# Convolution sums of a two-layer block: 20 of 31 taps added by accumulating DMAs, ten as multiply-adds on VectorE

## What is computed

```python
h = rms_norm(x, g_pre_mix) * (1 + sc1) + sh1       # sc1, sh1: from c @ w_ada + b_ada
proj = h @ w_in                                    # u_glu, q, k, v, index q and k, gates
a, gt = split(u_glu); u = a * sigmoid(gt)          # 256 x 1024
u = conv(u, w_dw, width 31, causal, one filter per channel) + b_dw
y_conv = silu(layer_norm(u, g_ln, b_ln)) @ w_conv_out
y_attn = top-k sparse attention, 16 heads of 64, @ w_attn_out
x = x + gt1 * rms_norm((g_conv * y_conv + g_attn * y_attn) @ w_o)
```

## Time and profile before

| | |
|---|---|
| Time of the runs | 2699.56 us median of 3 (2699.01 to 2699.8) |
| The profiled execution: its own time | 2699.8 us |
| Its span, first to last instruction | 2698.0 us |
| Mean granted TensorE clock | 0.988 of 2.4 GHz |
| TensorE matmuls busy | 2584.3 us, 96% |
| VectorE busy | 1684.5 us, 62% |
| ScalarE busy | 1286.2 us, 48% |
| GpSimd busy | 3.4 us |
| DMA | 579.29 MB, of them 564.82 MB on the queue of the loads |

### The profile page before, as it was taken

The page is one execution under the profiler, slowest core; times in us unless marked ns, Lnnn a source line. Parts: engine busy times, 40 slices in busy tenths (PEclk is TensorE's granted clock), DMA queues, the critical chain, the costliest instruction groups (busy, mean ns, idle before and its releaser), DMA issues.

```text
span 2698.0 us, 28994 instructions
## 1 busy us (share of the span) xinstructions
PE 2584.3 (96%) x11660; PEld 2111.5 (78%) x11660; DVE 1684.5 (62%) x1914; ACT 1286.2 (48%) x1797; POOL 3.4 (0%) x10
## 2 busy tenths in 40 slices
PE   4999989999989999999999899999999999999998
PEld 3777767877868888888888787778788888888886
DVE  6899788988875555555555544666554454445455
ACT  4535666755454444444444454544454444444443
POOL 0000000000000000000000000000000000000000
PEclk9999999999989999999999999999999999999999
DMA  9888445777855556665554554345455555555553
GB/s 352 326 332 324 157 156 197 270 281 278 342 222 203 218 204 234 241 242 212 209 205 176 180 186 158 141 156 187 172 177 195 187 195 197 188 194 194 188 187 125
DMA packets 80566, 579.29 MB, mean 215 GB/s; under 512 B 8964, under 2 KB 8964, under 8 KB 10544
## 3 DMA queue, kind: packets, MB, share of 16 engines
q1 hardware_dynamic: 78480, 564.82, 57.8%
q10 hardware_dynamic: 1440, 9.81, 0.9%
q0 software_dynamic: 512, 2.81, 0.3%
HBM read 573.73 MB, written 3.67 MB: 214 GB/s over the span
## 4 chain that ended last, share of the span: by engine, by line
PE 76%; DVE 7%; ACT 3%; issue 1%; DMA 0%; ACTq 0%; DVEq 0%; SPq 0%
PE bank L640 72%; DVE wlo L1459 2%; PE bank L604 1%; ACT whi L965 1%; DVE raw L1469 1%; DVE X L1454 1%; DVE cv L1664 1%; ACT PR L965 0%; DVE SS L1454 0%; DVE cv L1454 0%; PE bank L752 0%; PE bank L800 0%; ACT SS L1335 0%; DMA raw<-in_w_in 0%; PE bank L885 0%
## 5 line engine op out<-in xcount | busy, mean ns | idle before, releaser
L1459 DVE TENSOR_TENSOR wlo<-raw,whi 128x1024 fp32r<-128x1024 f32 x882 | 1077.3, 1224 | 957.1 <-ACT whi L965 953.4
L965 ACT ACTIVATE whi<-raw 128x1024 fp32r<-128x1024 f32 x882 | 932.3, 1059 | 1289.2 <-PE bank L640 1169.2
L640 PE MATMUL bank<-whi,HTh 128*128 128x512 f32 x2560 | 706.2, 398 | 8.8 <-ACT HTh L965 5.8
L640 PE MATMUL bank<-wlo,HTh 128*128 128x512 f32 x2560 | 687.6, 391 | 3.5 <-DVE wlo L1459 3.5
L640 PE MATMUL bank<-whi,HTl 128*128 128x512 f32 x2560 | 689.2, 391 | 0.5 <-DVE HTl L1775 0.5
L640 PEld LDWEIGHTS bank<-wlo,HTh 128*128 128x128 f32 x2560 | 481.6, 188 | 106.4 <-DVE wlo L1459 4.8
L640 PEld LDWEIGHTS bank<-whi,HTl 128*128 128x128 f32 x2560 | 483.5, 189 | 103.7 <-DVE HTl L1775 1.0
L640 PEld LDWEIGHTS bank<-whi,HTh 128*128 128x128 f32 x2560 | 472.5, 189 | 113.9 <-issue 15.6
L1469 DVE CUSTOM_DVE_ANT_0 raw<-raw,GT,VECS 128x2048 f32<-128x2048 f32 x96 | 225.0, 2347 | 0.2 <-DMA raw<-in_w_ada 0.2
L640 PE MATMUL bank<-whi,ACTh 128*128 128x512 f32 x704 | 191.6, 394 | 0.0
L640 PE MATMUL bank<-wlo,ACTh 128*128 128x512 f32 x704 | 190.0, 392 | 0.0
(11 more groups left out here) (217 smaller groups left out, 1235.5 us busy)
## 6 DMA issues: line engine op xcount, KB each, us to landing
raw<-in_w_in SPq DMA_DIRECT2D x128, 1024.0 KB, 4.9
raw<-in_w_ada SPq DMA_DIRECT2D x96, 1024.0 KB, 6.5
raw<-in_w_gate SPq DMA_DIRECT2D x88, 1024.0 KB, 4.8
raw<-in_w_up SPq DMA_DIRECT2D x88, 1024.0 KB, 4.8
raw<-in_w_down SPq DMA_DIRECT2D x88, 1024.0 KB, 4.8
raw<-in_w_o SPq DMA_DIRECT2D x16, 1024.0 KB, 7.0
raw<-in_w_out SPq DMA_DIRECT2D x16, 1024.0 KB, 4.8
raw<-in_w_attn_out SPq DMA_DIRECT2D x8, 1024.0 KB, 4.8
```

The costliest lines, as they stand in the source:

```text
L640: i = e.matmul(bank[2 * ch.st + t][:, :], (xl if ps == 1 else xh)[:, k, tk(t)], (lo if ps == 2 else hi)[:, j * 512:j * 512 + 512], start=c ...
L965: return e.activation(dst, src, ACT.Copy, scale=scale)
L1459: e.tensor_tensor(lo, src, r32(hi), S_).then_inc(lo_done, 1)
```

## The change

`ON_ACT` is replaced by `BY_DMA`, true for the 20 taps with j % 3 != 0. For those ScalarE writes the products into `PR[hf]` as before, and GpSimd issues a DMA that adds the 512 KB of `PR[hf]` to the half of `cv` (`accum_op=ALU.add`), 40 DMAs in all, each behind a wait for the products and one for the sum before. Each half has a semaphore, `cv_add`. The ten taps j = 3, 6, ..., 30 are multiply-adds on VectorE, each half behind the DMA of the tap before. ScalarE's products of tap j wait for the DMAs up to tap j - 1. The instruction of line 1664 is gone. The 40 DMAs stand in GpSimd's program between the store of `scratch` and the wait ahead of the load of `BT`.

```diff
@@ -349,6 +349,7 @@
     vec_in, c_in, row_in, rb_in, scr_in, bt_in, out_done = [
         S(n) for n in ("vec_in", "c_in", "row_in", "rb_in", "scr_in", "bt_in", "out_done")]
     x_in = [S(f"x{i}_in") for i in range(2)]
+    cv_add = [S(f"cv_add{hf}") for hf in range(2)]
     hi_done, lo_done, pe_done, pe_t0 = [S(n) for n in ("hi_done", "lo_done", "pe_done", "pe_t0")]
     emptied = {"ACT": S("act_emptied"), "DVE": S("dve_emptied")}
     ada_done = S("ada_done")
@@ -385,9 +386,9 @@
     att_dve = [steps(f"att{t}_dve", [(k, g) for g in R(4) for k in
                                      ("l0", "l1", "l2", "l3", "max", "rec", "norm", "lo")]) for t in R(2)]
     TAPS = [(j, hf) for j in R(KW) for hf in R(2)]
-    ON_ACT = [j % 4 != 3 for j in R(KW)]
-    cv_mul = steps("cv_mul", [(j, hf, i) for j, hf in TAPS if ON_ACT[j] for i in R(4)])
-    cv_dve = steps("cv_dve", ["pad", *[(j, hf, i) for j, hf in TAPS if j for i in R(1 if ON_ACT[j] else 4)],
+    BY_DMA = [j % 3 != 0 for j in R(KW)]
+    cv_mul = steps("cv_mul", [(j, hf, i) for j, hf in TAPS if j == 0 or BY_DMA[j] for i in R(4)])
+    cv_dve = steps("cv_dve", ["pad", *[(j, hf, i) for j, hf in TAPS if j and not BY_DMA[j] for i in R(4)],
                               "mu", "centre", "mean", "inv", "norm", *[("lo", c) for c in R(8)]])
     cv_pe = steps("cv_pe", ["sum", "sqsum"])
     cv_act = steps("cv_act", ["sq", "root", *[(k, c) for c in R(8) for k in ("silu", "hi")]])
@@ -540,6 +541,14 @@
     def conv_slot(n):
         return CONV0 + 4 * n // 3
 
+    def added(j, hf):
+        return cv_add[hf], 16 * sum(BY_DMA[:j + 1])
+
+    def conv_before(j, hf):
+        if j == 1:
+            return cv_mul(0, hf, 3)
+        return added(j - 1, hf) if BY_DMA[j - 1] else cv_dve(j - 1, hf, 3)
+
     GT_SLOT = [M["conv"] + 6, M["down01"] - 2]
     B0, B1, B2, B3 = M["ffn00"], M["in2"], M["ffn10"], M["end"]
     DIF0 = M["conv2"] - 10
@@ -758,7 +767,7 @@
                 yield 2
 
         def conv_sums():
-            w.wait_ge(*cv_dve(KW - 1, 1, 0))
+            w.wait_ge(*cv_dve(KW - 1, 1, 3))
             w.wait_ge(*att_dve[0]("lo", 3))
             for c in R(8):
                 i = e.matmul(bank[7][:, 0:T], ones[:, :], cv[:, c, :], start=c == 0, stop=c == 7)
@@ -1169,11 +1178,9 @@
             w.wait_ge(*rb_pe(7))
             w.wait_ge(*pro_dve("lam1"))
             for n, (j, hf) in enumerate(TAPS):
-                if ON_ACT[j]:
-                    if j:
-                        before = j - 1 if ON_ACT[j - 1] else j - 2
-                        if before > 0:
-                            w.wait_ge(*cv_dve(before, hf, 0))
+                if j == 0 or BY_DMA[j]:
+                    if j > 1:
+                        w.wait_ge(*added(j - 1, hf))
                     for i in R(4):
                         c = 4 * hf + i
                         src = uT[:, c, j:j + T]
@@ -1414,7 +1421,7 @@
             lane.begin(ATT0 + 5 * (t == 0), attend(t))
         lane.begin(CONV0, conv_products())
         lane.begin(SUM0 + 1, conv_act())
-        lane.begin(SUM0 + 2, row_load("g_post_mix", *[att_dve[t]("l3", 3) for t in R(2)], cv_dve(KW - 1, 1, 0)))
+        lane.begin(SUM0 + 2, row_load("g_post_mix", *[att_dve[t]("l3", 3) for t in R(2)], cv_dve(KW - 1, 1, 3)))
         for j in R(4):
             for t in R(2):
                 lane.begin(M["conv"] + 4 * j + 5 + t, mix_t(j, t))
@@ -1647,23 +1654,12 @@
             e.memset(uT[:, :, 0:KW - 1], 0.0).then_inc(*cv_dve.one("pad"))
             yield 1
 
-        def conv_before(j, hf):
-            if j > 1:
-                w.wait_ge(*cv_dve(j - 1, hf, 0 if ON_ACT[j - 1] else 3))
-            else:
-                w.wait_ge(*cv_mul(0, hf, 3))
-
         def conv():
             w.wait_ge(*tj_act("u4", 1))
             w.wait_ge(*cv_dve("pad"))
             for n, (j, hf) in enumerate(TAPS[2:]):
-                h4 = slice(4 * hf, 4 * hf + 4)
-                if ON_ACT[j]:
-                    w.wait_ge(*cv_mul(j, hf, 3))
-                    conv_before(j, hf)
-                    e.tensor_tensor(cv[:, h4, :], cv[:, h4, :], PR[hf][:, :, :], A_).then_inc(*cv_dve.one(j, hf, 0))
-                else:
-                    conv_before(j, hf)
+                if not BY_DMA[j]:
+                    w.wait_ge(*conv_before(j, hf))
                     for i in R(4):
                         c = 4 * hf + i
                         stt(cv[:, c, :], uT[:, c, j:j + T], vec("wdw", c * KW + j), cv[:, c, :], M_, A_).then_inc(
@@ -1991,6 +1987,11 @@
         e.dma_start(OH[0:33, :], A["onehot"]).then_inc(rb_in, 16)
         w.wait_ge(*rb_act(7))
         e.dma_start(A["scratch"], RD[:, :, :]).then_inc(scr_in, 16)
+        for j, hf in TAPS:
+            if BY_DMA[j]:
+                w.wait_ge(*cv_mul(j, hf, 3))
+                w.wait_ge(*conv_before(j, hf))
+                e.dma_start(cv[:, 4 * hf:4 * hf + 4, :], PR[hf][:, :, :], accum_op=ALU.add).then_inc(cv_add[hf], 16)
         w.wait_ge(scr_in, 16)
         w.wait_ge(pe_done, B1)
         e.dma_start(BT[:, :, :], bass.AP(A["scratch"].tensor, A["scratch"].offset + 127,
```

## The result

The changed kernel takes 2713.99 us, the median of 4 runs (2709.27 to 2717.09), against 2699.68 us of the kernel before: 0.53% or 14.3 us slower, ratio 1.0053 with a 95% interval of 1.0037 to 1.0069. The forecast was 2693.5 us, faster; 2713.99 lies inside the range, on the side of rivals B and C. All of them are under 1%, so each has to be read with its interval.

What follows compares the result with a forecast made beforehand. TensorE, busy 2584.3 of 2698.0 us, was taken as the bound, with 14.0 us of removable waits. The terms -7.2 + 0.7 + 0.5 = -6.0 us from 2699.8, with medians 0.24 lower, gave 2693.5 us; range 2687 to 2725.

Steps and rivals of the forecast that it cites:

- Rival B: Stage from 500 us: accumulates read twice on the load engines, loads late, 16 us lost, up to 2708 us; chance 0.25.
- C: Rival: ScalarE's wait for the second half's DMA, ten times, bounds beyond L = 9.1 us; 2715 at 11.4; chance 0.27.
- Work on VectorE and ScalarE: Convolution sums: 46 adds removed and 6 multiply-add halves more, VectorE net 43 us less; ScalarE's products 10.2 us less.
- Which waits shrink: TensorE's waits at the attention groups and from 500 us on: gains 1.8 + 4.0 + 1.1 + 0.3 = 7.2 us.
- The first group: First attention group, 336 to 360 us: VectorE's chain 1.84 us shorter, easing TensorE's waits for `wlo` and exponentials (3.69 us).
- the waits of 2.55 us: TensorE's waits at line 604's transposes, attention groups two and three: 2.0 us gained at each, down to 0.5.
- Room on the DMA engines: 500 to 571 us: loads need 55 us, twelve accumulates 16.2, 71.2 of 71 us; cost taken as 0.5 us.
- L = 6: Landing time in us of one 512 KB accumulating DMA from GpSimd's queue, taken between 3.8 and 11.4.
- The cover: Splits stand two slots ahead behind a stalled ScalarE product, leaving 4.4 us; landings up to 9.1 us cost nothing.
- The term of 0.7 us: Cost put in for places where exponentials stand behind a ScalarE stall on a landing.
- 2 L + 3.3: A half's chain of two landings, two products and a multiply-add; fills its 8 slots (28.5 us) at L = 12.6.
- Who waits: ScalarE's second product of a pair (tap 3k+2), second half: slack 4.7 us, stalls of 1.3 us, ten times.

## Why the prediction was wrong

- **Work on VectorE and ScalarE:** right. 42 and 10.2 us less busy, against 43 and 10.2.
- **Which waits shrink:** right in sum. 7.2 us forecast, 8.4 without the DMAs. The first group gave 1.83 us for 1.84, though not where it was looked for: the wait of 3.69 us was to fall to about 2 and is 4.02, and what shrank lies ahead of it. In the changed kernel itself the attention stage gave 4.7 of 6.9 us: the waits of 2.55 us fell to 0.55, but three new ones of 1.35, 0.50 and 0.30 us came at the transposes of the other 128 positions, and ScalarE stood 3.3 us behind landings before 480 us.
- **Room on the DMA engines: the step that failed.** It counted twelve times 0.524 MB once, at the rate of the saturated stretch 1.35 us each, and took 0.5 us for the cost. An accumulate takes 2.7 us of all 16 engines, the stage is some 10 us over (10 of them are issued in it, not 12), and DMAs of this kind that nobody waits for cost 13.8 us by themselves. The loads land late, ScalarE's splits wait for them, and TensorE waits for `whi`. Rival B had this mechanism, with 16 us as its price.
- **Landing time:** L = 6 was about right while there was room (5.3 us in the median from 290 to 340 us, 6.5 up to 480, with one of 12.6), and wrong where it mattered: 9.6 us from 500 us on, up to 11.4. The cover was said to hold to 9.1 us, and it broke there. The term of 0.7 us for it is too small with that. That a full stage lengthens the landings, so that B brings on C, was missed; the two stood as separate cases. The share of C is at most some 4 us: two buffers gave back 3.5, within the noise, and the late DMAs cost 18.4 us with ScalarE waiting for their landings, 13.8 with nobody waiting. One reading of the prediction is off too: its "2 L + 3.3" holds one product and one multiply-add (1.7 + 1.6), not the two products of its words.
- **Who waits:** the place was right, ScalarE's product of tap 3k+2; it lost 28.3 us there, 25 of them after 480 us.
- **The Trainium skill,** "Collectives: The Full Stack", section "The bandwidth ceiling: the fold count and why AG ≠ RS ≠ AR", says that an add in the DMA engines reads two sources on one ring and runs at half of a copy's rate. The page has it of reductions between ranks. The runs agree: 2.0 times a copy. The prediction gave the case that goes with it 0.25, and it is the one that came.

The sum as measured: -3.0 (gain below tap 19 with its DMAs) + 13.8 (late traffic) + 3.5 (one buffer in the late stage, not clear of noise) = 14.3 us, beside 14.3. That it closes so exactly is luck; each term has an interval of 2 to 4 us on either side, and the terms come from different kernels. It gives nothing to VectorE's relief in the late stage, where TensorE had only 0.3 us to gain.

## What to carry to other kernels

Before work is moved to DMAs, write the engines' time per stage next to the bytes: here an accumulating DMA took the time of two copies. The stage at a share of 0.86 had room for 8 of them and not for 16; the one at 0.51 took 24, and the kernel still gained 3.0 us of the 8.4 that it gains without them. Relief of a busy engine is worth only what stands directly ahead of the bound engine's waits; here moving the sums of every second tap of the early stage alone, and of tap 6 ahead of the first group, turned 14 us of loss into 8 us of gain. And a landing time taken from an idle stretch is not the one of the stretch in which it is waited for.

## What was unexpected of the hardware

- The queue's byte count shows an accumulate once (20.97 MB for 40 of 0.524), though its engine time is that of two copies: GB/s alone hide it. At a share of 1.00 the changed kernel moves 322 GB/s, the one with extra copies 369 at 0.97, and the earlier trace rows show 389 at 0.99.
- A DMA share of 1.0 does not by itself mean loss. With 8 extra DMAs it is 1.01 and TensorE is busy 70.9 of 71 us; ScalarE waits 12.0 us for `raw`, and the two pieces it is ahead cover it.
- The 1.9 us that the profiled changed kernel was behind at the first product of tap 1 are within the scatter: in the profiled executions of this study that product stands between 284.3 and 288.5 us, always ahead of the first changed work. Its runs also spread more, 2709 to 2717 us, where the kernel before stayed within 2699.0 to 2700.4 in the same runs; in later runs that one spread from 2696.5 to 2702.2.
